# Three changes to a hybrid decoder step: matmul order inside a tile, one convolution slot inside the samples' attention, and a padded block of constants

## The reference, cut to what matters

```python
xn = rmsnorm(x, norm_mix_g)
aq, ak, av, dq, dk, dvv, dz, da, db, ga, gb = split_cols(xn @ w_in, IN_SPLITS)
ya = swa_prompt(...)   or   swa_sample(...)      # window attention; the samples read a cache of 128 rows each
qkv = causal_dwconv(concat([dq, dk, dvv]), ...)  # the "dn" slots: 12 tiles of 128 columns
o, S = gated_delta(...); yb = rmsnorm(o) * silu(dz)
h = x + (sigmoid(ga) * (ya @ w_br_a) + sigmoid(gb) * (yb @ w_br_b)) @ w_mix_out
h = h + memory_attention(h) @ w_xo
u, gv = split(rmsnorm(h) @ w_up); h = h + (silu(causal_dwconv(u)) * gv) @ w_down   # d_ff = 2816
```

## Time and profile before

| | us |
|---|---|
| median of 3 runs (lowest, highest) | 1991.64 (1991.51, 1994.1) |
| the profiled execution | 1987.64 |
| its span, first to last instruction | 1985.8 |
| TensorE matmul busy in the span | 1875.2 |
| VectorE, ScalarE, GpSimd busy | 957.8, 489.5, 831.7 |

### The profile page before, as it was taken

How to read it: one execution, slowest core, us unless ns; L and a number is a source line. 1 busy time by engine, 2 the same in 40 slices (tenths; PEclk the granted TensorE clock), 3 DMA queues, 4 the chain that set the end, 5 groups by cost and what they waited for, 6 DMA issues and landing times.

```text
span 1985.8 us, 32389 instructions
## 1 busy us (share of the span) xinstructions
PE 1875.2 (94%) x13273; PEld 1767.8 (89%) x13273; DVE 957.8 (48%) x1150; ACT 489.5 (25%) x908; POOL 831.7 (42%) x907
## 2 busy tenths in 40 slices
PE   6988899999999899999999799999999999999997
PEld 6866799988887788998988699999999999999996
DVE  6877366764453231564141547344343444445346
ACT  6055326643222103412021533100010010000012
POOL 3411033331211223755664036555554555565465
PEclk9999999999999999999999999999999999999999
DMA  4311110110102121422222211111111111111112
GB/s 187 91 39 40 39 43 33 43 62 27 38 27 65 28 95 52 151 86 97 75 85 88 82 68 43 54 43 42 45 45 47 42 48 47 43 42 42 53 46 88
DMA packets 45483, 119.72 MB, mean 60 GB/s; under 512 B 3808, under 2 KB 20896, under 8 KB 44224
## 3 DMA queue, kind: packets, MB, share of 16 engines
q1 hardware_dynamic: 45392, 118.39, 17.9%
HBM read 102.94 MB, written 15.77 MB: 60 GB/s over the span
## 4 chain that ended last, share of the span: by engine, by line
PE 68%; DVE 7%; ACT 3%; issue 1%; POOL 0%; DVEq 0%; ACTq 0%; POOLq 0%
PE PS L544 42%; PE PS L1988 12%; PE PS L1378 3%; PE PS L1576 2%; PE PS L1870 1%; PE PS L1614 1%; PE PS L1770 1%; ACT TMP L1223 1%; DVE H L2651 1%; DVE XL L524 1%; PE PS L1935 1%; PE PS L2020 1%; PE PS L1661 0%; PE PS L1803 0%; DVE XL L2471 0%
## 5 line engine op out<-in xcount | busy, mean ns | idle before, releaser
L544 PE MATMUL PS<-XH,WH 128*128 128x352 f32 x2280 | 505.7, 330 | 34.2 <-POOL WL L759 14.0
L767 POOL TENSOR_TENSOR WH<-RAW,CST 128x256 fp32r<-128x256 f32 x288 | 195.2, 706 | 810.7 <-PE PS L544 409.3
L544 PE MATMUL PS<-XH,WL 128*128 128x352 f32 x2280 | 493.1, 324 | 0.0
L544 PE MATMUL PS<-XL,WH 128*128 128x352 f32 x2280 | 492.9, 324 | 0.0
L544 PEld LDWEIGHTS PS<-XH,WH 128*128 128x128 f32 x2280 | 389.3, 190 | 52.4 <-issue 34.9
L544 PEld LDWEIGHTS PS<-XH,WL 128*128 128x128 f32 x2280 | 392.8, 189 | 0.0
L544 PEld LDWEIGHTS PS<-XL,WH 128*128 128x128 f32 x2280 | 389.4, 189 | 0.0
L771 POOL TENSOR_TENSOR WL<-RAW,WH 128x256 fp32r<-128x256 f32 x288 | 260.6, 933 | 7.5
L2616 DVE TENSOR_TENSOR H<-H,PS 128x1056 f32<-128x1056 f32 x80 | 100.3, 1254 | 130.5 <-PE PS L1988 130.5
L757 POOL TENSOR_TENSOR WH<-RAW,CST 128x1024 fp32r<-128x1024 f32 x22 | 44.5, 2022 | 266.2 <-PE PS L544 139.7
L1285 ACT ACTIVATE AH<-TMP 128x1056 fp32r<-128x1056 f32 x20 | 20.8, 1081 | 359.0 <-PE PS L1988 345.5
(11 more groups left out here) (464 smaller groups left out, 2659.7 us busy)
## 6 DMA issues: line engine op xcount, KB each, us to landing
RAW<-in_w SPq DMA_DIRECT2D x136, 512.0 KB, 3.5
H<-in_xT SPq DMA_DIRECT2D x4, 1056.0 KB, 9.1
TMP<-in_xT SPq DMA_DIRECT2D x2, 2112.0 KB, 8.5
early_gates<-DV SPq DMA_DIRECT2D x18, 176.0 KB, 1.9
out_yT<-H SPq DMA_DIRECT2D x4, 704.0 KB
early_gates<-A SPq DMA_DIRECT2D x12, 176.0 KB, 1.8
DV<-early_gates SPq DMA_DIRECT2D x1, 2112.0 KB, 14.0
TMP<-early_gates SPq DMA_DIRECT2D x2, 1056.0 KB, 5.4
```

The lines of the kernel that those rows point to most:

```text
L544: mm = nc.tensor.matmul(PS[:, 3 * mm_g + c, 0:CW], w_[:, p, off + k * P:off + (k + 1) * P], x_[:, xk0 + k, c * CW:(c + 1) * CW], start=fir ...
L767: nc.gpsimd.tensor_tensor(WH[:, p, c], RAW[:, p, c], one[:, 0:PIECE], ALU.mult)
```

## The change

It does four things. In `gemm_part` and in `down` the loops over pairs and thirds change places: the thirds are outside, and the three pairs of one third follow each other into one bank. The first convolution slot is taken out of its place and cut into three parts (slices 0 to 2, 3 to 5 and 6 to 7) around the transposes and the value products of the samples' attention; for this the transposes go to banks 3 to 7 and the value products to bank 7, and ScalarE copies the last third of the gate rows before the transposes' results. The value products alternate between the two key-value groups, block by block. And CST is padded from 502 to 512 floats for each partition, so that AH, AL and A32 start at a multiple of 128 bytes.

```diff
-NCONST = _at
+NCONST = -(-_at // 64) * 64
...
-            for w_, x_ in ((WH, XH), (WH, XL), (WL, XH)):
-                for c in range(NCH):
+            for c in range(NCH):
+                for w_, x_ in ((WH, XH), (WH, XL), (WL, XH)):
...
             gate_rows(1)
+            gate_rows(2)
             for b in range(4):
                 act.wait_ge(ss_tp, b + 1)
...
-            gate_rows(2)
             act.wait_ge(ss_pv, 1)
...
             gate_products(2)
+
+            def dn_first(a, b):
+
+                for k in range(a, b):
+                    mm = gemm_part(0, 0, k, KT)
+                    if k == KT - 1:
+                        mm.then_inc(w_used, 1)
+            pe.wait_ge(w_split, SLOTS["dn"][0] + 1)
+            pe.wait_ge(acc_free, acc0["dn"])
+            pe.wait_ge(ss_msk, 2)
+            dn_first(0, 3)
             pe.wait_ge(ss_p, 1)
+            pe.wait_ge(ab_row, 3)
             for k in range(NB + 1):
...
+            dn_first(3, 6)
             pe.wait_ge(ss_pt, 5)
-            for g in range(2):
-                for k in range(NB):
-                    nc.tensor.matmul(PS[HD * g:HD * g + HD, 5, 0:CH], s_vc[:, k, HD * g:HD * g + HD], s_pt[:, k, g, :],
-                                     start=(k == 0), stop=False)
-                mm = nc.tensor.matmul(PS[HD * g:HD * g + HD, 5, 0:CH], s_v[0:TS, HD * g:HD * g + HD],
-                                      s_pt[0:TS, NB, g, :], start=False, stop=True)
+            for k in range(NB + 1):
+                for g in range(2):
+                    v = s_vc[:, k, HD * g:HD * g + HD] if k < NB else s_v[0:TS, HD * g:HD * g + HD]
+                    pt = s_pt[:, k, g, :] if k < NB else s_pt[0:TS, NB, g, :]
+                    mm = nc.tensor.matmul(PS[HD * g:HD * g + HD, 7, 256:256 + CH], v, pt, start=(k == 0), stop=(k == NB))
             mm.then_inc(ss_pv, 1)
-
-
-            pe.wait_ge(ab_row, 3)
+            dn_first(6, KT)
...
-            pe.wait_ge(ss_y, 1)
-            pe.wait_ge(ss_pt, 5)
...
-            dn_tile(0, 0, False)
             dn_tile(1, 1, False)
...
                     for k in range(2):
-                        for w_, x_ in ((WH, AH), (WH, AL), (WL, AH)):
-                            for c in range(NCH):
+                        for c in range(NCH):
+                            for w_, x_ in ((WH, AH), (WH, AL), (WL, AH)):
```

More of the change, by code:

```diff
@@ L906, in _ @@
                 nc.scalar.activation(s_pt[:, 2 * b:2 * b + 2, :, :],
-                                     PS[:, b, :].rearrange("p (k g n) -> p k g n", k=2, g=2),
+                                     PS[:, 3 + b, :].rearrange("p (k g n) -> p k g n", k=2, g=2),
                                      ACT.Copy).then_inc(ss_pt, 1)
             act.wait_ge(ss_tp, 5)
-            nc.scalar.activation(s_pt[0:TS, 8, :, :], PS[0:TS, 4, 0:256].rearrange("p (g n) -> p g n", g=2),
+            nc.scalar.activation(s_pt[0:TS, 8, :, :], PS[0:TS, 7, 0:256].rearrange("p (g n) -> p g n", g=2),
                                  ACT.Copy).then_inc(ss_pt, 1)
-            gate_rows(2)
             act.wait_ge(ss_pv, 1)
-            nc.scalar.activation(YA[:, :, TP:T], PS[:, 5, 0:CH].rearrange("p (j n) -> p j n", j=NJ),
+            nc.scalar.activation(YA[:, :, TP:T], PS[:, 7, 256:256 + CH].rearrange("p (j n) -> p j n", j=NJ),
                                  ACT.Copy).then_inc(ss_y, 1)
@@ L1453, in _ @@
                     i = 2 * k + g
-                    mm = nc.tensor.transpose(PS[0:rows, i // 4, (i % 4) * CH:(i % 4) * CH + CH],
+                    mm = nc.tensor.transpose(PS[0:rows, 3 + i // 4, (i % 4) * CH:(i % 4) * CH + CH],
                                              s_s[:, g, k * CH:k * CH + rows], ident)
@@ L2703, in layouts @@
              "w_ab": w_in[:, 2816:2824].reshape(KT, P, 8).transpose(1, 0, 2).reshape(P, 64)}
-    o["cst"] = A(np.concatenate([parts[k].astype(np.float32) for k in CONST], 1))
-    assert o["cst"].shape[1] == NCONST
+    o["cst"] = np.zeros((P, NCONST), np.float32)
+    for k, (a, n) in CONST.items():
+        o["cst"][:, a:a + n] = parts[k]
     pos = np.concatenate([np.arange(TP), np.tile(8192 + np.arange(LS), NB)]).astype(np.float32)
```

## The result

The changed kernel takes 1963.38 us (median of 4 runs, 1962.87 to 1966.77); the kernel before, run beside it, 1991.58 us (4 runs, 1989.93 to 1994.1). The ratio is 0.9861, interval 0.9844 to 0.9878: 1.4% faster. The profiled execution of the changed kernel took 1963.86 us with a span of 1962.1, so from profiled execution to profiled execution the gain is 1987.64 - 1963.86 = 23.8 us; from median to median it is 28.2 us, because the profiled execution of before lies 4 us under its median and this one 0.5 above its own. In the new code L1988 is L1997, L2020 is L2029, L1454 is L1466, L1461 is L1476, L1470 is L1482 and L1495 is L1504; L544, L1378 and L1395 stay.

A forecast was written before the change was run, and what follows sets the result against it. TensorE's matmul pace was taken as the bound, with practically no idle time in the MLP. Order 19.5 plus attention 5.2 made 24.7 us less: 1962.9 us profiled, 1966.9 us median, range 1958.7 to 1982.6.

The forecast's parts named there:

- the likeliest case: Whole kernel: loop order and attention gains both arrive, 24.7 us less; own range 1959 to 1975 us, chance 0.76.
- Part 1, the order: L544 and L1988 matmuls: new loop order brings 159.5 ns each, 19.5 us less, bounds 6.0 to 26.7.
- The runs of L1378: Early gates, already in the new order: runs of 158.6 to 161.2 ns, mean 159.5, taken as the new pace.
- Part 3, the padding: Constants and the buffers behind them: alignment worth 0 to 0.4 us, put at nothing.
- Part 2, the attention: Samples' attention: both waits filled and value products alternated, 5.2 us less, bounds 3.0 to 5.8.
- The waits less the changes of kind: Samples' attention: two TensorE waits go, 3.4 us, against 0.4 us for four more changes between kinds of matmul.
- the alternating products: Samples' attention: value products of the two groups overlap, 2.3 us instead of 4.5, 2.2 us less.
- The cover behind it: Behind the turned gate rows: ScalarE and VectorE chain stays 4.2 us, ending 7 us before TensorE wants it.
- The order gives nothing: Rival for the loop order: changing bank every three matmuls brings 161.9 ns back; 1986.4 us, chance 0.08.
- in part: Rival for the loop order: only the slowest gate runs' 161.2 ns is reached; 1980.4 us, chance 0.09.
- Slower by changes of bank: Rival: each change of bank costs a drained pipeline; 2022.1 us at 20 ns each, chance 0.04.
- The gain is lost to the gates' chain: Rival in the samples' attention: transposes, copies and chain come 7 us later than worked out; 1972.1 us, chance 0.03.

The follow-up runs named there:

- e6_oldaddr_onebank: Changed kernel with operands walked in the old order but three consecutive matmuls writing one bank, sums mixed; 1982.4 us.
- e3_pad: Kernel before with only the constants padded; 1986.19 us, ratio 0.9991, no difference that can be told.
- e1_order: Kernel before with only the two loop orders changed, no padding or new attention; 1977.9 us, ratio 0.994.
- e7_slot_back: Changed kernel with the first convolution slot whole again behind the attention, value products still alternating; 1963.6 us, one run.
- e8_groups_apart: Changed kernel with the value products one group after the other, slot still inside the attention; 1966.46 us, one run.
- e4: Changed kernel without the padding of the constants; 1970.31 us, ratio 0.991 against the kernel before.
- e9: Changed kernel with the pairs ordered (WH,XH), (WL,XH), (WH,XL); 1966.53 us, ratio 0.9894 against the kernel before.
- e12: Changed kernel with the thirds in the order 0, 2, 1; 1970.06 us, ratio 0.9923 against the kernel before.
- e2: Kernel before with only the samples' attention changed, old loop order and no padding; 1983.9 us, ratio 0.9975.
- e5: Changed kernel with the new operand order but each matmul writing the next of the tile's three banks, sums mixed; 1972.51 us.
- e10: Changed kernel with constants padded to 528 floats, so AH, AL and A32 start at 64 modulo 128 bytes; 1968.88 us.
- e11: Changed kernel with constants padded to 504 floats, so AH, AL and A32 start at 96 modulo 128 bytes; 1973.0 us.

## Why the prediction was right, and where it wasn't

**The sum.** Forecast were 24.7 us from one profiled execution to the other; 23.8 came, and by the medians 28.2 (the interval of the ratio makes it 24 to 31). The time of 1963.4 lies in the likeliest case's own range, and the mechanisms of parts 1 and 2 are the ones that the runs show. That the sum comes so close between the profiled executions is luck all the same: the order gave 3.0 us more than forecast, and the delta stage, which wasn't in the sum, took 3.75 us back. (The upper bound of part 1 adds up to 26.6 us, not 26.7; nothing hangs on it.)

**Part 1, the order: the size.** Taken were 159.5 ns; the MLP goes at 158.9, the mix stage (900 to 1050 us) at 160.0, the first tiles at 160.2. The MLP gained 13.8 us where "about 11" was forecast, and the rest of the order, from the table above with 0.4 us for the two slots next to the attention, 1.8 + 0.4 + 2.1 + 4.5 = 8.8; together 22.5 for 19.5. The runs of L1378 were a good copy because they keep to one third for the three pairs, as the new order does. For the bank and its changes, which the prediction carried along as a second possible reason and from which two rivals came, no run shows a part in it: e6_oldaddr_onebank keeps the old intervals with the new use of banks, and both patterns of the new sequence occur with banks used either way. Why the sequence of operands sets the pace is open.

**Part 3, the padding: the step that failed.** The prediction took from the earlier trace rows that L544 and L1988 differ by 0.3 ns, put the alignment at 0 to 0.4 us and chose nothing. That is right for the old order only (e3_pad: 0.3 ns). The rows couldn't show the other case, an unaligned operand in the new order, since the runs of L1378 that were taken as the copy all read aligned buffers. It is worth 4.2 ns x 1440 = 6.0 us, a quarter of the whole gain. Without it part 1 would have fallen short, 22.5 - 6.0 = 16.5 us for 19.5: in e1_order L1988 loses 1.0 ns where 2.7 were forecast as gain. The bound should have come from a sentence of its own: no row shows L1988's operands in the new order. Two edits priced apart hid a price that only exists for both.

**Part 2, the attention: right.** The waits less the changes of kind, 3.4 - 0.4 = 3.0, measured 3.08 (e7_slot_back; the two were not measured apart); the alternating products 2.2, measured 2.10 (e8_groups_apart); together 5.2 for 5.2. The gates' sums start 28.52 us after the last gate row, where 28.5 was forecast (257.9 - 229.41).

**The cover behind it: half used up by something not foreseen.** The prediction said that the gates' chain takes 4.2 us as in the earlier trace rows, and that POOL splits the next slot earlier, at nothing (a step that failed too, though it cost no time). Timeline of VectorE in the changed kernel:

```profile
244.86 1.07 DVE L2182 TENSOR_TENSOR TMP<-TMP,CST 128x36 f32<-128x36 f32 x1 [14.07 <-ACT TMP L921]
245.97 2.42 DVE L2183 TENSOR_SCALAR TMP<-TMP 128x36 f32<-128x36 f32 x1
248.42 0.20 DVE L2184 TENSOR_TENSOR TMP<-TMP 128x36 f32<-128x36 f32 x1
...
251.65 0.18 DVE L2192 TENSOR_TENSOR TMP<-TMP 32x32 f32<-32x32 f32 x1
```

and of POOL in the same stretch:

```profile
243.99 1.89 POOL L757 TENSOR_TENSOR WH<-RAW,CST 128x1024 fp32r<-128x1024 f32 x1 [25.72 <-PE PS L544]
245.97 2.38 POOL L759 TENSOR_TENSOR WL<-RAW,WH 128x1024 fp32r<-128x1024 f32 x1
```

Two instructions on 36 columns take 1.07 and 2.42 us and end within 0.05 us of POOL's two splits (245.93 and 245.88; 248.39 and 248.35). In e7_slot_back, where the slot comes back and POOL's split with it, the same two instructions are short; VectorE and POOL there:

```profile
236.05 0.20 DVE L2180 TENSOR_TENSOR TMP<-TMP,CST 128x36 f32<-128x36 f32 x1 [5.88 <-ACT TMP L921]
236.28 0.18 DVE L2181 TENSOR_SCALAR TMP<-TMP 128x36 f32<-128x36 f32 x1
```

```profile
247.43 1.89 POOL L757 TENSOR_TENSOR WH<-RAW,CST 128x1024 fp32r<-128x1024 f32 x1 [29.78 <-PE PS L544]
```

So the earlier slot frees the buffer earlier, POOL's split falls on the chain, and the chain, from ScalarE's first copy at 244.56 to the end of L2192, takes 251.83 - 244.56 = 7.3 us instead of 4.2. It cost nothing, since TensorE wants its result at 256.17; but of the 7 us of cover that the prediction gave only 4.3 are left. The Trainium skill ("SBUF — State Buffer", Who interferes with whom) says that a VectorE instruction with two inputs in SBUF, or in a mode that takes both ports, and a GpSimd instruction that reads SBUF hold a shared pair of ports against each other for their whole length. The trace agrees: both long instructions end with POOL's. The trace of the kernel before shows the same already, further on; its VectorE and POOL:

```profile
254.41 2.38 DVE L2211 TENSOR_SCALAR TMP<-TMP,CST 128x32 f32<-128x32 f32 x1
```

```profile
254.01 2.73 POOL L759 TENSOR_TENSOR WL<-RAW,WH 128x1024 fp32r<-128x1024 f32 x1
```

An instruction on 32 columns lasts 2.38 us and ends with POOL's split (256.79 and 256.74); in the changed kernel the same execution of it (L2220 at 253.41 us) takes 0.23. So the rule could have been applied ahead, to the one chain whose length the argument rested on. VectorE's 8.4 us of additional busy time come mainly from three places: 3.1 more in the chain, 4.3 less in all of L2211 / L2220, and 5.9 more in a copy of 16 columns, L2589 / L2598, of which ten take 0.75 us instead of 0.16; TensorE's pace in the MLP, without idle time, shows that they cost nothing there.

**The delta stage: not in the sum at all.** It lost 3.75 us. That isn't the change's doing, as far as the length of this stage (from L1520 / L1529 to L1743 / L1752) in fourteen profiled executions can show it:

| falls of the clock to 0.50 in the stage | executions | its length, us |
|---|---|---|
| none | before, e4, e6, e9, e12 | 260.3 to 260.4 |
| 3.4 us near 417 to 421 | e2, e5, e7 | 261.7 to 261.8 |
| 6.8 us near 419 | e8 | 263.1 |
| 6.8 us near 416 to 426 and 3.4 near 559 to 569 | after, e1, e3, e10, e11 | 264.0 |

The old order stands in the first line as in the last, and so do the new order and the new attention; e3_pad and e4_nopad, on one chip, stand in the last and in the first. Up to the fall the matmuls of the changed kernel's stage start as in e4_nopad's, to within 0.1 us. So by these traces the fall comes or doesn't come with the execution and not with the code. That one code spreads like this the kernel before shows as well: its 23 runs beside e1_order go from 1981.77 us at a mean granted clock of 0.996 to 1994.0 us at 0.988. The delta stage's falls are worth up to 3.7 us of such a difference, and a single profile can lie that far from the median of its kernel's runs.

**The rivals.** "The order gives nothing" and "in part" were ruled out by the pace in the MLP. "Slower by changes of bank" fell with it. "The gain is lost to the gates' chain" was nearer than it looked, at 4.3 us of cover for 7. Of the rules weighed ahead, columns / 2.4 + 2.5 ns for a single matmul (149.2 ns here, an estimate from the Trainium skill, "TensorE: Matmul & The Clock Gate", Back-to-back issue gap) has no term for what was found; the runs show 158.9 to 163.1 ns for the same instruction, by the sequence and place of its operands.

## What to carry to other kernels

Where TensorE is never idle, the interval from start to start is the time: read it to a tenth of a ns, for each line and in each stage, and look for a stretch of the same kernel in which the same instruction goes faster; its order of operands and the place of its buffers are the first things to copy, both together. Price two edits that touch the same operands together as well as apart, and say for which combination the trace has no row. When work is moved forward, look at what the other engines do earlier because of it, and lay that beside every chain whose length the argument rests on.

## What the runs showed of the hardware that wasn't expected

- The start-to-start time of a matmul of 352 columns in fp32r depends on the sequence of its operands: 161.8 ns with the thirds inside the pairs, 158.9 with the pairs inside the thirds. With the old sequence it is 161.8 or 161.9 whether the bank changes with every matmul or with every third (before, e6_oldaddr_onebank).
- In the new sequence it depends on where the moving operand starts: 158.9, 160.0, 163.1 and 163.1 ns at 0, 64, 88 and 96 modulo 128 bytes (64 and 96 in one execution each); in the old sequence 161.8 and 162.1 at 0 and 88.
- The same code on the same buffers has two patterns, 158.9 and 161.1 ns, fixed for a whole run of 288 matmuls. It is kept from run to run in the changed kernel (158.9) and in e5_newaddr_rotbank (161.1) and alternates in e10_off64. What chooses between them wasn't found.
- Products of 64 columns of weights that alternate between the two halves of the output's partitions run two at a time: 36 records in 2.26 us instead of 4.50.
- A VectorE instruction on 32 or 36 columns took 2.38 or 2.42 us instead of 0.23 or 0.18 beside a split on GpSimd, and ended with it within 0.05 us; the profile shows the wait as busy time.
- The granted clock falls to 0.50 for 3.4 or 6.8 us in some executions and not in others with the same work; in the delta stage that costs 1.4 to 3.7 us.
